# The second mixer's entry: one scale for two norms, the angles inside the feed-forward, the residual's norm moved to the output projections

## What is computed

```python
h = h + 0.5 * swiglu_ffn(rmsnorm(h, ffn2_norm), ffn2_w_in, ffn2_w_out)
x = rmsnorm(h, final_norm)                        # first block's result

cos, sin = rope_tables(positions)                 # angles of 256 positions x 32 frequencies
mod = silu(c) @ w_ada + b_ada                     # 6 vectors of 1024
shift1, scale1, gate1, shift2, scale2, gate2 = split(mod, 6)
h = rms_norm(x, g_pre_mix) * (1.0 + scale1) + shift1
y = token_mixer(h, cos, sin, ...)                 # projections w_in, a convolution of 31 taps, attention,
                                                  # attn_out, conv_out and w_out
x = x + gate1 * rms_norm(y, g_post_mix)
# rms_norm(x, g): x * rsqrt(mean(x*x) + 1e-6) * g, the mean over the 1024 columns
```

## Time and profile before

| | |
|---|---|
| median of three runs | 1147.13 us (1144.88 to 1148.12) |
| the profiled execution | 1146.29 us, span 1144.5 us |
| mean granted clock of TensorE | 0.954 |
| busy TensorE, VectorE, ScalarE, GpSimd | 93%, 73%, 41%, 42% of the span |
| second feed-forward's loop | 452.8 to 628 us |
| last down slab, entry, first projection ends | 629.3, 635.3 to 650.5, 659.9 us |
| attention and convolution | about 724 to 853 us |

### The profile page before, as it was taken

How to read it: one execution, slowest core, us unless ns; L and a number is a source line. 1 busy time by engine, 2 the same in 40 slices (tenths; PEclk the granted TensorE clock), 3 DMA queues, 4 the chain that set the end, 5 groups by cost and what they waited for, 6 DMA issues and landing times.

```text
span 1144.5 us, 19795 instructions
## 1 busy us (share of the span) xinstructions
PE 1060.9 (93%) x8149; PEld 1017.5 (89%) x8149; DVE 840.2 (73%) x835; ACT 472.3 (41%) x508; POOL 481.9 (42%) x312
## 2 busy tenths in 40 slices
PE   6999999798798989999999799999799969999996
PEld 6999999796688978999999699986689959999995
DVE  4987677899669559687777859999977475555554
ACT  4434333444150245343333444553466443333332
POOL 1667676402209121375766789998800010000001
PEclk9999999898699999999999899997799979999998
DMA  9767767645431035768677336472225515555521
GB/s 326 226 214 247 240 215 256 184 142 159 141 106 42 1 110 186 234 207 265 208 257 238 98 122 186 112 218 74 74 94 165 177 44 160 180 188 178 189 96 37
DMA packets 165130, 188.81 MB, mean 165 GB/s; under 512 B 10478, under 2 KB 154428, under 8 KB 164956
## 3 DMA queue, kind: packets, MB, share of 16 engines
q1 hardware_dynamic: 164112, 185.91, 51.0%
q0 software_dynamic: 192, 1.88, 0.4%
q10 hardware_dynamic: 780, 0.37, 0.2%
HBM read 187.10 MB, written 1.05 MB: 164 GB/s over the span
## 4 chain that ended last, share of the span: by engine, by line
PE 73%; DVE 18%; ACT 3%; issue 3%; DMA 2%; SPq 1%; DVEq 0%; ACTq 0%
PE ps L1693 46%; PE ps L1707 17%; DVE wl L1085 3%; DVE ps L1445 3%; PE ps L1843 3%; ACT wh L686 2%; DMA raw<-in_ffn_w_in 2%; DVE work L1207 2%; PE ps L1721 1%; PE ps L1827 1%; DVE rstd L1106 1%; PE ps L1819 1%; DVE yl L1096 1%; PE ps L1732 1%; PE ps L1777 1%
## 5 line engine op out<-in xcount | busy, mean ns | idle before, releaser
L1693 PE MATMUL ps<-xh,wh 128*128 128x256 f32 x1272 | 373.3, 293 | 19.1 <-DVE xl L1429 6.3
L1693 PE MATMUL ps<-xl,wh 128*128 128x256 f32 x1272 | 367.5, 289 | 0.0
L1693 PE MATMUL ps<-xh,wl 128*128 128x256 f32 x1272 | 367.1, 289 | 0.0
L1090 DVE TENSOR_TENSOR wl<-raw,wh 128x2048 fp32r<-128x2048 f32 x84 | 245.7, 2925 | 72.5 <-ACT wh L692 72.5
L1693 PEld LDWEIGHTS ps<-xh,wh 128*128 128x128 f32 x1272 | 251.5, 198 | 26.9 <-issue 17.8
L1693 PEld LDWEIGHTS ps<-xl,wh 128*128 128x128 f32 x1272 | 252.1, 198 | 0.1
L1693 PEld LDWEIGHTS ps<-xh,wl 128*128 128x128 f32 x1272 | 251.9, 198 | 0.0
L692 ACT ACTIVATE wh<-raw 128x2048 fp32r<-128x2048 f32 x84 | 160.5, 1911 | 156.4 <-PE ps L1693 156.4
L1085 DVE TENSOR_TENSOR wl<-raw,wh 128x2048 fp32r<-128x2048 f32 (+1 forms) x69 | 165.2, 2399 | 48.6 <-ACT wh L686 48.1
L565 POOL TENSOR_TENSOR ada_raw<-ada_raw,c_act 128x2048 f32<-128x2048 f32 x24 | 90.0, 3751 | 261.9 <-DMA ada_raw<-in_w_ada 244.8
L686 ACT ACTIVATE wh<-raw 128x2048 fp32r<-128x2048 f32 (+1 forms) x69 | 129.6, 1878 | 135.0 <-PE ps L1693 110.4
(11 more groups left out here) (319 smaller groups left out, 1690.1 us busy)
## 6 DMA issues: line engine op xcount, KB each, us to landing
raw<-in_ffn_w_in SPq DMA_DIRECT2D x44, 1024.0 KB, 7.4
ada_raw<-in_w_ada SPq DMA_DIRECT2D x24, 1024.0 KB, 5.3
raw<-in_ffn_w_out SPq DMA_DIRECT2D x22, 1024.0 KB, 4.9
raw<-in_w_in SPq DMA_DIRECT2D x18, 1024.0 KB, 5.4
raw<-in_w_mlp_in SPq DMA_DIRECT2D x16, 1024.0 KB, 5.5
raw<-in_w_mlp_out SPq DMA_DIRECT2D x16, 1024.0 KB, 4.9
raw<-in_w_mix_in SPq DMA_DIRECT2D x14, 1024.0 KB, 5.4
raw<-in_w_mix_out SPq DMA_DIRECT2D x4, 1024.0 KB, 5.0
```

Source lines behind the costliest of these rows:

```text
L1090: dve.tensor_tensor(wl[:, s % SLOTS, :], raw[:, s % SLOTS, :], wh[:, s % SLOTS, :].bitcast(F32), ALU.subtract).then_inc(low_done, 1)
L1693: mm = pe.matmul(bank[:, m * T:(m + 1) * T], w[:, k, m * P:(m + 1) * P], r[:, k, :], start=(m == 0 and k == 0 and j == 0), stop=(k == KT - ...
```

## The change

- Sums: only the squares of resid times final_coef are summed ahead of the mixer, with final_coef = sqrt(final_norm^2 + 1e-6). The factor of both norms together is 1/sqrt(mean + 1e-12) of these sums (eps_sq): x's own norm cancels out of the second, and what its two epsilons leave is in the coefficient. The factor, scale, is written by the reciprocal to PSUM.
- u = resid x mods[0] (with final_norm inside) is made in ffn's end, pair by pair; then kn = u x scale by pairs.
- The modulation vectors are made after the last low part of the feed-forward, ahead of the residual's last additions; VectorE's subtraction of the second glu slab stands behind these, that of the third behind the low tiles. ScalarE's cast of the third stands behind the high tiles.
- The first glu projection goes by tile: both halves of the slab for each tile.
- The residual's own sums (f) come after the high and low tiles: GpSimd squares, TensorE sums after the second glu projection, ScalarE keeps them in std. Their root and reciprocal and the product with resid and final_norm stand in attn_out.
- GpSimd waits for the whole residual of the first mixer and its norm's sums (mix_resid, n3_tiles), loads the positions, does step 14, the sine's angles, step 15, the cosine's, and then steps 16 to 23. The work arrays of the angles lie in w_v.

```diff
@@ GpSimd
             modulation(FF_STEPS + 2)
-            with pool.Fori(0, FF_STEPS - 1) as i:
-                modulation(i + (FF_STEPS - 1 + ADA_MIX))
-            squares("f", "ffn2_resid", kn)
-
-            pool.wait_ge(*at("ffn2_resid", 4))
-            pool.memset(upad[:, :, 0:PAD], 0.0).then_inc(S("upads"), 1)
-
+
+            pool.wait_ge(*at("mix_resid", 4))
+            pool.wait_ge(*at("n3_tiles", 1))
             pool.dma_start(cosines.bitcast(I32), a["positions_2"].to_broadcast([P, T])).then_inc(S("pos_loaded"), 16)
...
-            ang, turns, part = tap_mem[:, 0, :], tap_mem[:, 1, :], w_v[:, 0:T]
+            ang, turns, part = (w_v[:, n * T:(n + 1) * T] for n in range(3))
...
+            modulation(FF_STEPS - 1 + ADA_MIX)
+            pool.memset(upad[:, :, 0:PAD], 0.0).then_inc(S("upads"), 1)
             pool.wait_ge(*at("pos_loaded", 16))
-            pool.wait_ge(*at("ada_taken", ADA_STEPS))
             step(pool.tensor_copy(ang, cosines.bitcast(I32)))
...
                 else:
                     step(ins)
-            pool.wait_ge(*at("angles", 1))
+                    modulation(FF_STEPS + ADA_MIX)
+            with pool.Fori(0, FF_STEPS - 3) as i:
+                modulation(i + (FF_STEPS + 1 + ADA_MIX))
+
+            pool.wait_ge(*at("h_xl", 8))
+            squares("f", "ffn2_resid", f_squares)
+            pool.wait_ge(*at("ada_taken", ADA_STEPS))
@@ ScalarE
                 if name == "ffn2":
-                    cast(s0 + 3 * FF_STEPS + 2)
+
+                    act.wait_ge(*at("final_sq", 1))
+                    act.activation(final_coef, final_sq, ACT.Sqrt, bias=eps).then_inc(S("final_coef"), 1)
+                    act.wait_ge(*at("final_coef", 1))
...
-                act.activation(qn[:, t, :], resid[:, t, :], ACT.Square, scale=col("final_norm", t)).then_inc(S("fg_sq"), 1)
-            root("f", ps[6][:, 0:T], std[:, :], D)
-            act.wait_ge(*at("m2", 1))
-            act.activation(kr, kr_raw, ACT.Sqrt, scale=1.0 / D, bias=eps).then_inc(S("g_std"), 1)
+                act.activation(qn[:, t, :], resid[:, t, :], ACT.Square, scale=final_coef[:, t:t + 1]).then_inc(S("fg_sq"), 1)
+
+            act.wait_ge(*at("g_stat", 1))
+            act.activation(std[:, :], ps[6][:, 0:T], ACT.Sqrt, scale=1.0 / D, bias=eps_sq).then_inc(S("g_std"), 1)
             for t in range(KT):
-                act.wait_ge(*at("h_f", t + 1))
+                act.wait_ge(*at("h_f", t // 2 + 1))
                 act.activation(xh[:, t, :], kn[:, t, :], ACT.Identity, bias=ada[:, t:t + 1]).then_inc(S("h_xh"), 1)
+            cast(FIRST["glu"] + 2)
             for n in range(4):
                 s = FIRST["glu"] + 2 * n
                 cast(s + 3)
+                if n == 1:
+
+                    act.wait_ge(*at("g_rstd", 1))
+                    act.wait_ge(*at("f_stat", 1))
+                    act.activation(std[:, :], ps[1][:, 0:T], ACT.Copy).then_inc(S("f_kept"), 1)
...
-            root("ln", ps[1][:, 0:T], std[:, :], D)
+            root("ln", ps[1][:, 0:T], kr_raw, D)
+            act.wait_ge(*at("f_kept", 1))
+            act.activation(std[:, :], std[:, :], ACT.Sqrt, scale=1.0 / D, bias=eps).then_inc(S("f_std"), 1)
@@ VectorE: ffn, and behind it
+            def modulation_vectors():
...
+                dve.tensor_tensor(final_sq, vecs("final_norm"), vecs("final_norm"), ALU.mult).then_inc(S("final_sq"), 1)
+                dve.wait_ge(*at("ada_taken", ADA_STEPS))
...
-                with dve.Fori(0, FF_STEPS - 1) as i:
+                with dve.Fori(0, FF_STEPS - 2) as i:
...
+                if name == "ffn1":
+                    sub(s + 5)
+                else:
+                    modulation_vectors()
...
+                    if name == "ffn2":
+                        dve.wait_ge(*at("ffn2_resid", b + 1))
+                        for t in (2 * b, 2 * b + 1):
+                            ins = dve.tensor_scalar(kn[:, t, :], resid[:, t, :], mods[:, 0, t:t + 1], None, ALU.mult)
+                        ins.then_inc(S("h_u"), 1)
                 if name == "ffn2":
-                    sub(s + 3)
+                    sub(s + 2)
...
+            scale = ps[6][:, T:2 * T]
+            dve.wait_ge(*at("h_u", 4))
+            inverse("g", scale, std[:, :])
...
+            for b in range(4):
+                dve.tensor_tensor(kn[:, 2 * b:2 * b + 2, :], kn[:, 2 * b:2 * b + 2, :], spread(scale, 2), ALU.mult)\
+                    .then_inc(S("h_f"), 1)
+                if b:
+                    low_pair(b - 1)
+            low_pair(3)
+            sub(FIRST["glu"] + 2)
             dve.wait_ge(*at("upads", 1))
...
             sub(s + 6)
+            inverse("f", std[:, :], std[:, :])
+            for t in range(KT):
+                dve.scalar_tensor_tensor(resid[:, t, :], resid[:, t, :], col("final_norm", t), std[:, :], ALU.mult, ALU.mult)
@@ TensorE
+                order = [(m, k) for k in inputs for m in range(m_tiles)] if by_tile else \
+                    [(m, k) for m in range(m_tiles) for k in inputs]
...
-            column_sums("f", lambda k: kn[:, k, :], KT, ps[6][:, 0:T], ("f_sq", 1), by_pair=True)
-            column_sums("f", lambda k: qn[:, k, :], KT, ps[5][:, 0:T], ("fg_sq", 8))
+            for k in range(KT):
+                pe.wait_ge(*at("fg_sq", k + 1))
+                mm = pe.matmul(ps[6][:, 0:T], ones, qn[:, k, :], start=(k == 0), stop=(k == KT - 1), skip_group_check=True)
+            mm.then_inc(S("g_stat"), 1)
...
-                wide(s, ps[4 + 2 * (n % 2)], xh, xl, "h_xl" if n == 0 else None, one)
+                wide(s, ps[4 + 2 * (n % 2)], xh, xl, "h_xl" if n == 0 else None, one, by_tile=(n == 0))
                 wide(s + 1, ps[5 + 2 * (n % 2)], xh, xl)
+                if n == 0:
+                    column_sums("f", lambda k: f_squares[:, k, :], KT, ps[1][:, 0:T], ("f_sq", 1), by_pair=True)
```

More of the change, by code:

```diff
@@ L58 @@
 C = {}
-for _name, _width in (("ident", P), ("ones", P), ("eps", 1), ("inv_freq", 1), ("qk_scale", 1), ("swap", P),
+for _name, _width in (("ident", P), ("ones", P), ("eps", 1), ("eps_sq", 1), ("inv_freq", 1), ("qk_scale", 1), ("swap", P),
                       ("causal", 3 * P), ("upper", P), ("levels", LEVELS * P), ("row_of", 64), ("grp_row_of", 32),
@@ L1156, in ffn @@
                     sub_in_loop(s + 5, i, 3)
+                s = s0 + 3 * FF_STEPS - 4
+                gate(s, FF_STEPS)
+                sub(s + 3)
+                up(s + 1, FF_STEPS)
+                sub(s + 4)
+                hidden(FF_STEPS)
+                rest(FF_STEPS)
+                if name == "ffn1":
+                    sub(s + 5)
+                else:
+                    modulation_vectors()
                 s = s0 + 3 * FF_STEPS - 1
@@ L1419, in _ @@
-            st.sync()
-            dve.wait_ge(*at("x2_scaled", KT))
-            for n in range(KT + 2):
-                if n < KT:
-                    dve.scalar_tensor_tensor(kn[:, n, :], resid[:, n, :], mods[:, 0, n:n + 1], hid[:, 0, 0:T], ALU.mult,
-                                             ALU.mult).then_inc(S("h_f"), 1)
-                t = n - 2
-                if t < 0:
-                    continue
-                dve.wait_ge(*at("h_xh", t + 1))
-                dve.scalar_tensor_tensor(xl[:, t, :], kn[:, t, :], ada[:, t:t + 1], xh[:, t, :].bitcast(F32), ALU.add,
-                                         ALU.subtract).then_inc(S("h_xl"), 1)
@@ L1681, in _, with wide @@
         def _(pe):
-            def wide(s, bank, x, y, tile_ready=None, tile_base=0, slab=None, m_tiles=2, inputs=range(KT)):
+            def wide(s, bank, x, y, tile_ready=None, tile_base=0, slab=None, m_tiles=2, inputs=range(KT),
+                     by_tile=False):
                 slab = s if slab is None else slab
@@ L1687, in wide @@
                 h, l = (w[:, slab % SLOTS, 0:n].rearrange("p (k m) -> p k m", k=KT) for w in (wh, wl))
-                for m in range(m_tiles):
-                    for k in inputs:
-                        if tile_ready is not None and m == 0:
-                            pe.wait_ge(*at(tile_ready, tile_base(k)))
-                        for j, (w, r) in enumerate(((h, x), (h, y), (l, x))):
-                            mm = pe.matmul(bank[:, m * T:(m + 1) * T], w[:, k, m * P:(m + 1) * P], r[:, k, :],
-                                           start=(m == 0 and k == 0 and j == 0), stop=(k == KT - 1 and j == 2),
-                                           skip_group_check=True)
+                order = [(m, k) for k in inputs for m in range(m_tiles)] if by_tile else \
+                    [(m, k) for m in range(m_tiles) for k in inputs]
+                for m, k in order:
+                    if tile_ready is not None and m == 0:
+                        pe.wait_ge(*at(tile_ready, tile_base(k)))
+                    for j, (w, r) in enumerate(((h, x), (h, y), (l, x))):
+                        mm = pe.matmul(bank[:, m * T:(m + 1) * T], w[:, k, m * P:(m + 1) * P], r[:, k, :],
```

(2 more changed lines are left out.)

60 lines of the change are left out of this document (27 added, 33 removed).

## The result

The median after is 1150.53 us (20 executions, 1146.98 to 1154.12) against 1147.44 for before (20 executions, 1142.96 to 1150.83). The ratio is 1.0032, 95% interval [1.0022, 1.0043]: 2.5 to 4.9 us slower. The forecast was 1156, 1143 to 1168. The sign is right and the time lies in the range, but the loss is about a third of the one forecast.

A forecast was written before the change was run, and what follows sets the result against it. TensorE was taken as the bound, with idle GpSimd not spare because its w_ada chain had little margin. Loop +13.7, last down slab -1.1, entry -4.85 and final norm +1.0 gave +8.75, so 1156 us, range 1143 to 1168.

The forecast's parts named there:

- The angles stretch and step 16 is late: Second feed-forward's loop: beside VectorE's subtractions the angles take 32.2 us, so step 16 ends at 514.0, asked for at 504.94.
- At 17.9 us each ... I take 18.2 ... +13.7: Loop: seven more w_ada steps at 18.2 us make the last result ready at 641.4 against 627.66, +13.7 us.
- the drift: Loop: w_ada steps take 17.9 us against TensorE's 17.5, so the margin shrinks and lateness is never made up.
- Rival 3: Loop: step 16 ends at 517.6 and each later step takes 18.9 us; +17.25, median 1164.4 us; chance 0.25.
- By the rule: Loop: GpSimd's instructions and VectorE's two-input ones block each other for their whole length, so step 16 ends at 517.6.
- The last down slab's -1.1: Loop's end: after such a stall the last down slab need not wait 1.1 us for the hidden low part.
- The entry: -4.85: From the last down slab to the mixer's projections: a shorter chain, less the residual's own sums, -4.85 us in all.
- The chain's -7.55: Entry: with the slab cast and other work off the chain, the first projection matmul comes at 643.0 instead of 650.55.
- The own sums' +3.65: Entry: the residual's own sums move behind the second projection, where TensorE is the bound, +3.65 us.
- The clock and the order by tile: Entry: first projections by tile, at half clock for 6.4 us, take 14.3 us against 15.3, -0.95.
- Final norm in attn_out: +1.0: attn_out: a reciprocal and eight products on VectorE make the subtractions queued behind 5 us late; +1.0, bounds 0 and 4.
- Rival 1: Loop: the angles fit, step 16 ends by 503 and the margin holds; -5.75, median 1141.4 us; chance 0.14.

The follow-up runs named there:

- e3: The changed kernel with one line moved: GpSimd's step 14 back ahead of its two waits, angles still between steps 14, 15 and 16; 1145.36 us, ratio 0.9978.
- e10: e3 with w_ada's steps from 17 on alternating between two buffers; 1142.39 us, ratio 0.9960.
- e12: The changed kernel with 14 and 30 unread matmuls on TensorE ahead of its waits for steps 15 and 16; 1149.61 us, ratio 1.0019.
- e2: The kernel before with only GpSimd's new order, entry and final norm as before; 1155.22 us, ratio 1.0059.
- e4: The changed kernel with TensorE taking each w_ada result of the second feed-forward one round on, ahead of the down slab; 1150.22 us, ratio 1.0024.
- e11: e4 with w_ada's steps from 17 on alternating between two buffers; 1144.22 us, ratio 0.9977.
- e1: The changed kernel with step 14 back beside mix_out and all angles out of the loop, behind step 23; 1141.12 us, ratio 0.9931.
- e8: e1 with the residual's squares, then all angles, behind the low tiles; 1148.05 us, ratio 0.9997.
- e9: e5 with GpSimd squaring the residual directly behind step 23, ahead of all the angles; 1140.86 us, ratio 0.9948.
- e5: e1 with the residual's squares between the angles' halves and its sums in the hole ahead of the first projection; 1139.45 us, ratio 0.9917.

## Why the prediction was right, and where its size was wrong

1. *The angles stretch and step 16 is late: right.* Forecast 514.0, found 512.3, with waits at the ends of the second and third round as named. Within the sum, the angles took 17.1 + 11.4 = 28.5 us instead of 32.2, the three reductions 37.8 instead of 36.6 and the 0.7 reckoned ahead of them (step 14 alone took 13.3), and GpSimd began at 449.87, 445.0 in before's time, instead of 443.5. Mix_out had given 1.0 us instead of 1.9: its idle of 1.88 went, but the reduce behind it began only 1.0 earlier (445.41 - 4.88 = 440.53 against 441.55). That the sum came within 1.7 us is partly luck, since the angles' error and the others' have opposite signs.
2. *"At 17.9 us each ... I take 18.2 ... +13.7": this is the step that failed.* The term should have been +9.3. I took step 23's end for the time of TensorE's last sum. But behind step 16 TensorE waited for no step any more. The seven steps behind it took 121.6 us (517.16 to 638.78), 17.4 each, because step 17 was a short one of 15.7 (its second instruction 2.40 us and not 4.33), and the others took 17.65. With the slow round of 19.3 that gave TensorE a margin of 3.8 us at step 17 (532.88 against 536.65), of which 3.0 was left at step 23 (638.78 against 641.81). Of the 4.4 us between +13.7 and +9.3, 1.6 is step 16's earlier end; the rest is this: in place of the 4.7 us of drift in my sum (seven steps of 18.2 against rounds of 17.5) there was +1.8 of clock. The 17.9 was a poor average as well: before's own last three steps took 17.7 each, and only the ones ahead of them 18.0 to 18.2. The text had the branch that came true: "If the wait is there but the rounds after it stay at 17.5, the drift is wrong, and 1151 or less would be the result."
3. *The drift itself is real, though.* In e3, where the margin is near zero, each round goes at the chain's pace, and with a second buffer the rounds behind step 16 take 1.1 us less in all (e10). After escaped it through its margin, to which the short step 17 gave 1.9 us and its own slow round 1.8. That was luck in part: in e12, with the same order on GpSimd and as slow a round, step 17 took 19.3 us, and the margin was 0.2. Rival 3, steps of 18.9 one after the other, appeared nowhere; single steps as long did (that one, and step 22 of e2 with 19.8). By the rule (the Trainium skill, SBUF — State Buffer, Who interferes with whom) step 16 would have ended at 517.6; it ended at 512.3. The trace agrees that single instructions are held for nearly as long as a subtraction of 2.3 us (3.00, 2.99 and 3.15 us for some of 1.07), but not that it meets every one.
4. *The last down slab's -1.1: wrong.* The wait for fl is 1.11 us after as before. Rounds at the usual pace had come in between.
5. *The entry: -4.85 forecast, -6.3 found.* The chain's -7.55 is exact, with 1.76 us for the reciprocal into PSUM and the 4.3 us hole as worked out. The own sums' +3.65 is 3.3. The clock and the order by tile gave -2.0 instead of -0.95 (the 15.3 us that I set against were 15.1). I had carried over the time to 657 from the earlier trace rows, but the clock had been low since 647 there, within a hole of 6.3 us; in after's hole of 4.3 it fell only when the work began again, and was low for 3.4 us. Here too luck had a part: in e3, e4, e10 and e11, behind the same hole, it was low for 6.8 us, and the projections gained 0.8 to 1.3.
6. *Final norm in attn_out: +1.0 forecast.* TensorE's wait there is 0.38 us, and all behind the entry together comes to 0.0. It is next to nothing:

```profile
889.10 0.38 PE L1725 MATMUL ps<-xh,wh 128*128 128x256 f32 x1 [0.38 <-DVE work L1622]
```

Summed: the loop, with point 4, was forecast at +12.6 and is +9.3; the entry is 1.5 better; the norm 1.0 better. That is the 5.8 us between +8.75 and +2.9.

Rival 1's time, 1141.4, is that of e1, 1141.1, but by other shares: e1's profile has 4.2 us of gain in the entry, none in mix_out and 0.7 lost behind the entry. The agreement of the totals is not evidence for the terms.

## What to carry to other kernels

An engine that is idle half of the time may still have no time to give: what counts is the margin between the moment its result is ready and the moment it is asked for, and whether anything makes lateness up. With a single buffer whose pace equals the loop's, only a step that happens to be short does; in e10 and e11 a second buffer did.

When a late result stops TensorE, price it from the moment the result is ready, and only for that result. The waits ahead of it and what the clock loses in them are already inside, the clock behind it comes on top, and the later results need their own comparison of ready against asked.

Work is cheap in a hole of its engine only if it leaves the engines beside it alone and makes nothing behind it later: the angles cost 9.3 us in the loop and 0.9 to 2.1 beside the entry, and behind the entry they delayed the convolution, which cost 6.9 (e8 less e1).

## What the runs showed of the hardware

The granted clock fell behind quite short waits of TensorE: behind 1.95 (e4 and e11), 2.26 (e12), 2.27, 4.21 and 4.31 (after) and 2.29 us (e9), each time to the lower level, 1.2 GHz, and for 3.4 us in all, which costs 1.7 to 1.8 us. Behind 3.58 us followed by 1.07 (e4's end), behind the hole of 5.22 (e1) and behind the entry's hole of 4.3 in e3, e4, e10 and e11 it was low for 6.8. It did not fall behind waits of 1.03 (e10), 1.10 (the wait for fl), 1.72 (e11), 1.88 (before, at 432.92) and 2.01 (e3, at 433.55), nor in e5, where the hole is broken into 1.67 and 1.52 us by four matmuls. So the length of a wait alone doesn't tell what it costs: nearly equal ones cost nothing or 1.7 us, and equal ones 1.7 or 3.4. In the entry of after it fell only at about 658, when TensorE had been at work again for 0.8 us. I had expected a cost only for the long hole.

A VectorE product of a tile with a column of scalars (128x256, one input in SBUF) took 0.31 us alone (after) and 0.67 to 0.75 beside GpSimd (e1's first pair, e9). I had counted on VectorE's two-input instructions alone. The Trainium skill says so too (SBUF — State Buffer, Who interferes with whom): such an instruction can enter a mode in which it needs the port pair that it shares with GpSimd.
